# A chunked delta-rule recurrence moved to 64x64 array tiles and interleaved across sequence tiles

## The chip, the cores and the metric

One Trainium2 chip, one of its cores. The metric is the device time of one execution of the whole program in microseconds (us), the median of the runs. All arithmetic of the part that changes is fp32.

## What is computed

The program is a forward pass over 512 tokens of width 1024: a block with an RWKV-7 time mixing beside a differential attention, a cross attention, and further mixers and MLPs. The change touches only the recurrence of RWKV-7, for 8 heads of 64 dimensions:

```
def step(state, inp):
    r_t, w_t, k_t, v_t, kk_t, a_t = inp
    sa = jnp.einsum("bhvk,bhk->bhv", state, -kk_t)
    state = (state * w_t[:, :, None, :]
             + sa[..., None] * (kk_t * a_t)[:, :, None, :]
             + v_t[..., None] * k_t[:, :, None, :])
    y = jnp.einsum("bhvk,bhk->bhv", state, r_t)
    return state, y
```

Both kernels compute it in chunks of 64 tokens. Within a chunk the 64 steps are one linear system per head, a unit triangular 64x64 matrix whose inverse is built by doubling: from blocks of 1 to blocks of 2, 4, 8, 16, 32, 64. The first doubling is a mask; the other five are the "levels" `l = 0..4`, with matrix products. The state passes from chunk to chunk in order.

## The kernel before

Five engines run hand-written streams that wait for each other by counting semaphores. TensorE (the profile's PE) multiplies into eight PSUM banks PB0 to PB7, VectorE (DVE) and ScalarE (ACT) carry results from PSUM to the planes of one large buffer AR, GpSimd (POOL) splits streamed weights for the large projections. A 128 x 512 plane of AR holds, for a tile of 128 tokens, four pairs of heads; `t` is one of the four tiles and has the chunks `c = 2t, 2t+1`; `q` is a head's half of the pair. The helpers `mm` (line 1451) and `tr` (1454) issue one matmul and one transpose; all DVE operations of the stage come from `tt` (line 847), all of ACT's from `f` (line 404), so the trace shows them under lines 1452, 1455, 847 and 404. Each fp32 `mm` is two pairs of records, a weight load and a matmul; I call such a pair a pass. A transpose is one pass.

The recurrence stands between the differential attention and a group norm, with nothing else beside it: a loop over the four tiles, in PE's stream, in DVE's (under `for t in range(TT)`, after three memsets of the state) and in ACT's, each ending in `end_stage()`, where the three engines drain and wait for each other.

Within a tile PE issues: 16 transposes (alpha, v, the decayed beta and k) into PB4 to PB7, which ACT evicts as `TOKA, TOKV, TOKB, TOKK`; 40 products over 64 rows (`head_products` and those for the transposed matrix), which DVE masks into `AQ, BQ, TI, UI`; five levels; `P1`, `TA` and `W1`; the two state steps; and the output `y`, which ACT copies to `HN`. The inverse is kept twice, as `TI` and transposed as `UI`. Both chunks of a head lie as two 64x64 blocks on the diagonal of a 128x128 matrix whose other blocks are zero, so each level multiplies 128x128 matrices, one per head:

```
last = mm(bank4(q, e), AQ[:, h, 0:P], TI[:, h, :])
last = mm(bank4(2 + q, e), UI[:, h, :], XI[:, h, :])
last = mm(bank4(4 + q, e), XI[:, h, :], UI[:, h, :])
```

For half q = 0 and then q = 1, DVE masks the first product to `XI`, and subtracts the other two from `TI` and `UI`. A state step is, for chunk c: read the state `GS[c % 3]` by `TA` (`sa_mm`), form the innovation `SA` on DVE (`sa_ev`), add `TOKK x TOKV` and `TOKB x SA` in PB1 (`gu_mm`), and add the faded state `TG` on DVE (`g_ev`).

Of the kernel before, what the change touches and what calls it, by code (L numbers as in the profile page):

```python
# [20 lines left out]
ACT = mybir.ActivationFunctionType  # L21
# [26 lines left out]
for _name, _n in STREAM:  # L48
# [8 lines left out]
          ("bd_strict", 128), ("bd_incl", 128), ("low_mask", 6 * 128), ("gla_mask", 8 * 128),  # L57
# [32 lines left out]
def constants():  # L90
# [13 lines left out]
    def rope(name, head, width):  # L104
# [5 lines left out]
        for base in range(0, P, width):  # L110
# [13 lines left out]
    same = row // 64 == col // 64  # L124
    put("bd_strict", (same & (row < col)) * 1.0)
    put("bd_incl", (same & (row <= col)) * 1.0)

    low = [((row // (2 * s) == col // (2 * s)) & (row % (2 * s) >= s) & (col % (2 * s) < s)) * 1.0
           for s in (1, 2, 4, 8, 16, 32)]
    put("low_mask", np.concatenate(low, 1))  # L130
# [29 lines left out]
def build(nc, x_d, mem_d, w_d, c_d, v_d, out_d):  # L160
    ctx = ExitStack()
    with ctx:
# [5 lines left out]
        def sb_both(name, shape):  # L168
# [23 lines left out]
                 "ch_trev", "ch_aq", "ch_aqev", "ch_t0ev", "lv_x", "lv_xev", "lv_y", "lv_yev", "w1_mm", "w1_ev", "g_ev", "sa_mm",  # L192
# [74 lines left out]
        AQ, BQ = pk(41, 4, 256), pk(45, 4, 256)  # L267
        TI, UI, XI = pk(49, 2, 128), pk(51, 2, 128), pk(53, 2, 128)
        TOKA, TOKB, TOKK, TOKV = (pk(a, 1, 128) for a in (55, 56, 57, 58))
        BP, KP = pk(59, 1, 128), pk(60, 1, 128)  # L270
        TA, W1, SA, P1 = pk(39, 1, 128), pk(40, 1, 128), pk(18, 1, 128), pk(14 + 7, 1, 128)
        GS = [pk(a, 1, 128) for a in (15, 16, 17)]
        TG = pk(19, 1, 128)

# [118 lines left out]
        def _(act):  # L393
# [140 lines left out]

            for t in range(TT):
                for n, dst in enumerate((TOKA, TOKV, TOKB, TOKK)):
                    act.wait_ge(sems["ch_tr"], 4 * t + n + 1)
                    f(dst, PB[4 + n][:, :].rearrange("p (a n) -> p a n", n=P), ACT.Copy).then_inc(*A.inc("ch_trev"))
                act.wait_ge(sems["w1_mm"], 3 * t + 1)
                f(P1, PB[7][:, :].rearrange("p (a n) -> p a n", n=P), ACT.Copy).then_inc(*A.inc("w1_ev"))  # L540
                act.wait_ge(sems["w1_mm"], 3 * t + 2)
                f(TA, PB[5][:, :].rearrange("p (a n) -> p a n", n=P), ACT.Copy).then_inc(*A.inc("w1_ev"))
                act.wait_ge(sems["w1_mm"], 3 * t + 3)
# [293 lines left out]
        def _(dve):  # L837
# [202 lines left out]

            def two(bank):
                return PB[bank][:, :].rearrange("p (a n) -> p a n", n=256)

            def four(bank):
                return PB[bank][:, :].rearrange("p (a n) -> p a n", n=P)

# [1128 lines left out]
```

## Time and profile before

| what | value |
|---|---|
| median of 3 runs | 2532.34 us (2530.25 to 2533.34) |
| the profiled execution: its time / its span | 2532.6 us / 2530.8 us |
| PE busy | 2306.1 us, 91% of the span |
| DVE, ACT, POOL busy | 1131.1, 583.6, 1192.1 us (45%, 23%, 47%) |
| DMA | 182.52 MB, mean 72 GB/s |

The span goes from the first instruction to the last; the execution's own time is 1.8 us longer. Busy times are of one profiled execution. In a row of the trace, `128*64 128x128` behind a PE operation is the stationary operand (rows*columns) and the moving one (partitions x columns); PEld is the weight load, which has its own column of busy time. The time of a merged row of matmuls ends with the last result, so it is longer than the passes' issue.

### The profile page before, as it was taken

How to read it: one execution, taken by the hardware profiler on the slowest of the kernel's cores; microseconds unless marked ns; L12 is line 12 of the kernel's file. 1: busy time of each engine (PE TensorE's matmuls, PEld its weight loads, DVE VectorE, ACT ScalarE, POOL GpSimd, SP SyncE). 2: the span in 40 equal slices, each digit the busy share in tenths (PEclk: the TensorE clock that was granted, in tenths of full speed). 3: DMA queues.
4: the chain of work that ended last, by engine and by line, in shares of the span. 5: the costliest groups of instructions: out<-in, count | busy, mean ns of one | idle time of the engine just before them, and what ended most of it. 6: DMA issues, size and time to landing. Idle time of an engine off the chain costs nothing.

```text
span 2530.8 us, 28962 instructions
## 1 busy us (share of the span) xinstructions
PE 2306.1 (91%) x11270; PEld 1878.9 (74%) x11270; DVE 1131.1 (45%) x1566; ACT 583.6 (23%) x1161; POOL 1192.1 (47%) x660
## 2 busy tenths in 40 slices
PE   7996788859799999999788779999999998999999
PEld 5763688848678888887466658888887776888887
DVE  6775555552335311336588855311333555530220
ACT  3234200031232200211222152200213554210110
POOL 4550000026625766765223316666665433666665
PEclk9997799989999999999889899999999999999999
DMA  4220000012212232232111102232232121222222
GB/s 185 84 75 17 1 1 1 1 44 99 92 50 79 97 100 93 98 100 84 50 42 42 50 17 82 93 100 95 96 100 84 59 67 36 98 95 96 100 92 90
DMA packets 49641, 182.52 MB, mean 72 GB/s; under 512 B 5504, under 2 KB 5632, under 8 KB 49280
## 3 DMA queue, kind: packets, MB, share of 16 engines
q1 hardware_dynamic: 49248, 179.30, 21.4%
q8 instruction: 72, 1.18, 0.2%
q10 hardware_dynamic: 288, 1.77, 0.2%
q14 instruction: 33, 0.27, 0.0%
HBM read 178.95 MB, written 2.10 MB: 72 GB/s over the span
## 4 chain that ended last, share of the span: by engine, by line
PE 78%; DVE 14%; ACT 5%; issue 2%; POOL 1%; DMA 0%; ACTq 0%; DVEq 0%; SPq 0%; POOLq 0%
PE PB L1488 20%; PE PB L1489 20%; PE PB L1491 20%; PE PB L1452 14%; DVE AR L847 6%; ACT AR L404 4%; PE PB L1455 1%; PE PB L1470 1%; DVE AR L850 1%; PE PB L1545 1%; DVE HN L850 1%; DVE AR L1263 1%; DVE SM L1260 1%; DVE AR L854 1%; DVE SM L890 1%
## 5 line engine op out<-in xcount | busy, mean ns | idle before, releaser
L386 POOL TENSOR_SCALAR WH<-W 128x1024 fp32r<-128x1024 f32 x328 | 354.3, 1080 | 1300.8 <-PE PB L1491 817.9
L1489 PE MATMUL PB<-AR_r,WL 128*128 128x512 f32 (+1 forms) x2496 | 965.8, 388 | 0.0
L388 POOL TENSOR_TENSOR WL<-W,WH 128x1024 fp32r<-128x1024 f32 x328 | 838.0, 2555 | 27.4
L1491 PE MATMUL PB<-AR_r,WH 128*128 128x512 f32 (+1 forms) x2496 | 606.6, 385 | 0.0
L1489 PEld LDWEIGHTS PB<-AR_r,WL 128*128 128x128 f32 x2496 | 476.4, 191 | 100.3 <-issue 7.3
L1491 PEld LDWEIGHTS PB<-AR_r,WH 128*128 128x128 f32 x2496 | 464.1, 189 | 93.0
L1488 PE MATMUL PB<-HN_r,WH 128*128 128x512 f32 x1256 | 511.4, 407 | 0.6 <-POOL WL L388 0.6
L1488 PE MATMUL PB<-AR_r,WH 128*128 128x512 f32 (+1 forms) x1240 | 471.6, 383 | 12.7 <-ACT AR L404 8.1
L1452 PE MATMUL PB<-AR 128*128 128x128 f32 (+6 forms) x2848 | 398.6, 316 | 69.2 <-ACT AR L404 39.9
L1452 PEld LDWEIGHTS PB<-AR 128*128 128x128 f32 (+2 forms) x2848 | 335.6, 201 | 109.4 <-issue 35.8
L404 ACT ACTIVATE AR<-AR 128x512 f32<-128x512 f32 (+4 forms) x278 | 161.0, 616 | 830.3 <-DVE AR L850 729.5
L847 DVE TENSOR_TENSOR H<-H,PB 128x512 f32<-128x512 f32 x80 | 55.0, 687 | 522.3 <-PE PB L1491 485.6
L1488 PEld LDWEIGHTS PB<-HN_r,WH 128*128 128x128 f32 x1256 | 241.0, 192 | 60.8 <-issue 10.5
L850 DVE SCALAR_TENSOR_TENSOR AR<-PB,AR 128x512 f32<-128x512 f32 (+3 forms) x145 | 93.5, 645 | 427.9 <-PE PB L1491 383.1
L1488 PEld LDWEIGHTS PB<-AR_r,WH 128*128 128x128 f32 x1240 | 236.1, 190 | 58.8 <-ACT AR L404 10.1
L847 DVE TENSOR_TENSOR AR<-AR 128x512 f32<-128x512 f32 (+2 forms) x160 | 228.1, 1444 | 45.3 <-ACT AR L404 42.1
L404 ACT ACTIVATE AR<-PB 128x256 f32<-128x256 f32 (+3 forms) x293 | 131.8, 483 | 430.1 <-PE PB L1452 204.2
L847 DVE TENSOR_TENSOR AR_r<-AR,AR_r 128x512 fp32r<-128x512 f32 (+1 forms) x120 | 138.7, 1163 | 12.6 <-ACT AR_r L404 12.6
L1455 PE MATMUL PB<-C,AR 128*128 128x128 f32 x364 | 67.9, 305 | 73.8 <-ACT AR L404 49.1
L1455 PEld LDWEIGHTS PB<-C,AR 128*128 128x128 f32 x364 | 45.6, 153 | 111.1 <-issue 30.6
L1452 PE MATMUL PB<-AR,C 128*128 128x512 f32 x132 | 72.9, 652 | 49.3 <-DVE AR L847 36.9
L404 ACT ACTIVATE AR<-PB,SM 128x128 f32<-128x128 f32 (+3 forms) x128 | 51.0, 447 | 164.6 <-DVE SM L890 87.1
(100 smaller groups left out, 1144.0 us busy)
## 6 DMA issues: line engine op xcount, KB each, us to landing
W<-weights_in SPq DMA_DIRECT2D x328, 512.0 KB, 3.4
C<-constants_in SPq DMA_DIRECT2D x1, 2976.0 KB, 17.1
H<-x_in SPq DMA_DIRECT2D x4, 512.0 KB, 6.8
h_out<-H SPq DMA_DIRECT2D x8, 256.0 KB, 4.4
AR<-mem_in ACTq DMA_DIRECT2D x1, 1024.0 KB, 4.8
V<-vectors_in ACTq DMA_DIRECT2D x1, 703.0 KB, 4.5
C<-constants_in SPq DMA_DIRECT2D x1, 68.0 KB, 3.9
```

Source lines behind the costliest of these rows:

```text
L386: pool.tensor_scalar(WH[:, u % 2, :], w, 1.0, 1.0, ALU.mult, ALU.mult).then_inc(sems["w_round"], 1)
L388: pool.tensor_tensor(WL[:, u % 2, :], w, WH[:, u % 2, :].bitcast(F32), ALU.subtract)\
L404: return act.activation(out, in_, func, **k)
L847: return dve.tensor_tensor(out, a, b, op)
L850: return dve.scalar_tensor_tensor(out, a, scalar, b, op0, op1)
L854: return dve.tensor_scalar(out, a, s1, None, op0)
L890: return dve.tensor_reduce(out, in_, AX.X, op, negate=negate)
L1452: return pe.matmul(out, lhsT, rhs, start=start, stop=stop, **k)
L1455: return pe.transpose(out, in_, cst("ident"))
L1488: pe.matmul(out, lh, rl, start=start and k == 0, stop=False)
L1489: pe.matmul(out, ll, rh, start=False, stop=False)
L1491: ins = pe.matmul(out, lhs(k)[0], rhs(k)[0], start=False, stop=stop and k == KT - 1)
```

## The change

Everything stays fp32 and the stage stays where it is; the other stages are untouched, except that the constants have other masks (5568 columns in the second transfer in place of 5952).

- The two chunks no longer share a 128x128 matrix. Every matmul of the tile's products, the levels, `P1`, `TA`, `W1` and the inner part of `y` is a 64x64 stationary block against 64 moving columns. The inverse `T` of a chunk lies in the partition half opposite to its transpose `U`, so that `corner` (the first product of a level) reads half 1-c and writes half c, and `widen` (the other two) uses all four quadrants of the array. Planes `TU_[t % 2]` and the next hold T and U, `X_` holds 1 - X, `L_` the masked corners.
- `correction` forms 1 - X on DVE from PSUM, and `widen` multiplies T and U by it, so that its results are the new T and U whole; ACT copies them (`level_ev`), T first. `lower` (DVE) masks the level's corner of the matrix in SBUF, ahead of time.
- Operands are doubled by tile parity. The next tile's products (`first_products`, `a_products`, `b_products`) and transposes (`tokens`), and the last tile's state steps (`state_read`, `state_add`) and output (`y_chunk`, `y_state`) stand between the levels. The `end_stage` barriers within the stage are gone, with semaphores in their place.

The diff, cut:

```diff
+        def sub(plane, half, n):
+            return AR[64 * half:64 * half + 64, plane, 64 * n:64 * n + 64]
...
+            def level_ev(t, l):
+                act.wait_ge(sems["lv_tu"], 5 * t + l + 1)
+                if l < 4:
+                    f(AR[:, TU_[t % 2], :], PB[1][:, :], ACT.Copy).then_inc(*A.inc("lv_tev"))
+                f(AR[:, TU_[t % 2] + 1, :], PB[2][:, :], ACT.Copy).then_inc(*A.inc("lv_uev"))
...
+                level_ev(t, 0)
+                level_ev(t, 1)
+                if t < 3:
+                    tokens_ev(t + 1, 0, 7)
+                level_ev(t, 2)
+                if t:
+                    y_evict(t - 1)
+                level_ev(t, 3)
+                if t < 3:
+                    for n in range(1, 4):
+                        tokens_ev(t + 1, n, (7, 3, 7, 5)[n])
+                act.wait_ge(sems["p1_mm"], t + 1)
+                f(P1, PB[6][:, :].rearrange("p (a n) -> p a n", n=P), ACT.Copy).then_inc(*A.inc("p1_ev"))
+                level_ev(t, 4)
+                act.wait_ge(sems["ta_mm"], t + 1)
+                for c in range(2):
+                    f(TA[:, 4 * c:4 * c + 4, :], PB[4 + c][:, 0:256].rearrange("p (a n) -> p a n", n=64), ACT.Copy)\
+                        .then_inc(*A.inc("ta_ev"))
+                act.wait_ge(sems["w1_mm"], t + 1)
+                f(W1, PB[2][:, :].rearrange("p (a n) -> p a n", n=P), ACT.Copy, scale=-1.0).then_inc(*A.inc("w1_ev"))
+            y_evict(TT - 1)
...
+            def first_inverse(t):
+                dve.wait_ge(sems["tu_mm"], t + 1)
+                dst = [AR[:, TU_[t % 2]:TU_[t % 2] + 2, 256 * q:256 * q + 256].rearrange("p k (e n) -> p k e n", n=64) for q in range(2)]
+                for q in range(2):
+                    tt(dst[q], quads(PB[5 + q][:, :], 2), pair_mask("m_low0"), ALU.mult).then_inc(*D.inc())
                 dve.wait_ge(*D.latest)
                 for q in range(2):
-                    tt(heads4(TI, q), eye, heads4(TI, q), ALU.subtract).then_inc(*D.inc("ch_t0ev"))
-                for q in range(2):
-                    tt(heads4(UI, q), AQ[:, q::2, 0:P], pairt, ALU.mult).then_inc(*D.inc())
+                    tt(dst[q], eye24, dst[q], ALU.subtract).then_inc(*D.inc("tu_in"))
+            def lower(t, l):
+                dve.wait_ge(sems["aq_ev"], 2 * t + 2)
+                m = cst("m_up", 64 * l, 64 * l + 64).unsqueeze(1).unsqueeze(1).to_broadcast([P, 2, 4, 64])
+                tt(quads(AR[:, L_[l % 2], :], 2), AR[:, AQ_[t % 2]:AQ_[t % 2] + 2, 0:256].rearrange("p k (e n) -> p k e n", n=64), m,
+                   ALU.mult).then_inc(*D.inc("l_in"))
+            def correction(t, l):
+                dve.wait_ge(sems["lv_x"], 5 * t + l + 1)
+                tt(AR[:, X_, :].rearrange("p (a n) -> p a n", n=64), eye8, PB[0][:, :].rearrange("p (a n) -> p a n", n=64), ALU.subtract)\
+                    .then_inc(*D.inc("lv_xev"))
...
+                fade(c + 1)
+                dve.wait_ge(*D.latest)
+            fade(0)
+            decays(0)
+            first_inverse(0)
+            masked(0, "aq", AQ_[0], (3, 7), "m_strict")
+            lower(0, 0)
+            masked(0, "bq", BQ_[0], (1, 6), "m_strict")
+            for t in range(TT):
+                correction(t, 0)
+                if t:
+                    innovation(2 * t - 2)
+                lower(t, 1)
+                if t < 3:
+                    first_inverse(t + 1)
+                correction(t, 1)
+                if t:
+                    next_state(2 * t - 2)
+                lower(t, 2)
+                if t:
+                    innovation(2 * t - 1)
+                correction(t, 2)
+                lower(t, 3)
+                if t < 3:
+                    decays(t + 1)
+                if t:
+                    next_state(2 * t - 1)
+                correction(t, 3)
+                lower(t, 4)
+                correction(t, 4)
+                if t < 3:
+                    masked(t + 1, "aq", AQ_[(t + 1) % 2], (3, 7), "m_strict")
+                    lower(t + 1, 0)
+                    masked(t + 1, "bq", BQ_[(t + 1) % 2], (1, 6), "m_strict")
+            innovation(6)
+            next_state(6)
+            innovation(7)
...
+            def chunk_products(t, name, banks, ev, *kinds):
+                take(banks[0])
+                take(banks[1])
+                for e in range(4):
+                    for k, (lhs, rhs, swap) in enumerate(kinds):
+                        for c in range(2):
+                            half = 1 - c if swap else c
+                            for q in range(2):
+                                r, o = slice(64 * q, 64 * q + 64), 256 * k + 64 * e
+                                last = mm(PB[banks[q]][64 * half:64 * half + 64, o:o + 64], lhs(e, t)[r, 64 * c:64 * c + 64],
+                                          rhs(e, t)[r, 64 * c:64 * c + 64])
+                last.then_inc(*T.inc(name))
+                free[banks[0]], free[banks[1]] = ev
+            key, query = (lambda p, t: px(K0 + p, t)), (lambda p, t: px(R0 + p, t))
+            def first_products(t):
+                chunk_products(t, "tu_mm", (5, 6), [("tu_in", 2 * t + 2)] * 2, (alpha, beta, True), (beta, alpha, False))
+            def a_products(t):
+                chunk_products(t, "aq_mm", (3, 7), [("aq_ev", 2 * t + 1), ("aq_ev", 2 * t + 2)], (beta, alpha, True), (beta, query, False))
+            def b_products(t):
+                chunk_products(t, "bq_mm", (1, 6), [("bq_ev", 2 * t + 1), ("bq_ev", 2 * t + 2)], (key, alpha, False), (key, query, False))
+            def corner(t, l):
+                pe.wait_ge(sems["l_in"], 5 * t + l + 1)
+                pe.wait_ge(*((sems["tu_in"], 2 * t + 2) if l == 0 else (sems["lv_tev"], 4 * t + l)))
+                take(0)
+                for n in range(8):
+                    for c in range(2):
+                        last = mm(PB[0][64 * c:64 * c + 64, 64 * n:64 * n + 64], sub(L_[l % 2], 1 - c, n), sub(TU_[t % 2], 1 - c, n))
+                last.then_inc(*T.inc("lv_x"))
+                free[0] = ("lv_xev", 5 * t + l + 1)
+            def widen(t, l):
+                pe.wait_ge(sems["lv_xev"], 5 * t + l + 1)
+                if l:
+                    pe.wait_ge(sems["lv_uev"], 5 * t + l)
+                take(1)
+                take(2)
+                u = TU_[t % 2] + 1
+                for n in range(8):
+                    if l < 4:
+                        for c in range(2):
+                            mm(PB[1][64 - 64 * c:128 - 64 * c, 64 * n:64 * n + 64], sub(u, c, n), sub(X_, c, n))
+                    for c in range(2):
+                        last = mm(PB[2][64 * c:64 * c + 64, 64 * n:64 * n + 64], sub(X_, c, n), sub(u, c, n))
+                last.then_inc(*T.inc("lv_tu"))
+                if l < 4:
+                    free[1] = ("lv_tev", 4 * t + l + 1)
+                free[2] = ("lv_uev", 5 * t + l + 1)
...
+            first_products(0)
+            for n in range(4):
+                tokens(0, n, (7, 3, 7, 5)[n])
+            a_products(0)
+            b_products(0)
             for t in range(TT):
...
-                end_stage()
+                corner(t, 0)
+                if t:
+                    state_read(2 * t - 2)
+                widen(t, 0)
+                if t < 3:
+                    first_products(t + 1)
+                corner(t, 1)
+                if t:
+                    state_add(2 * t - 2)
+                widen(t, 1)
+                if t:
+                    state_read(2 * t - 1)
+                corner(t, 2)
+                if t < 3:
+                    tokens(t + 1, 0, 7)
+                widen(t, 2)
+                if t:
+                    state_add(2 * t - 1)
+                    y_chunk(t - 1)
+                corner(t, 3)
+                if t:
+                    y_state(t - 1)
+                widen(t, 3)
+                if t < 3:
+                    tokens(t + 1, 1, 3)
+                    tokens(t + 1, 2, 7)
+                corner(t, 4)
+                if t < 3:
+                    tokens(t + 1, 3, 5)
+                value_terms(t)
+                widen(t, 4)
+                if t < 3:
+                    a_products(t + 1)
+                solved_alpha(t)
+                if t < 3:
+                    b_products(t + 1)
+                solved_values(t)
+            state_read(6)
+            state_add(6)
+            state_read(7)
+            y_chunk(3)
+            y_state(3)
+            pe.wait_ge(sems["y_ev"], 8)
+            for b in range(4):
+                take(b)
             for p in range(4):
```

Where the instructions went. First PE, in the levels of a middle tile, one row per run of equal matmuls (`64x64` is the output, partitions x columns; lv_x and the like are the semaphores waited for). Before, one level:

```order
L1452 MATMUL PB0<-AR 128x128 [waits lv_yev]
L1452 MATMUL PB0<-AR 128x128 x3
L1452 MATMUL PB1<-AR 128x128 [waits lv_yev]
L1452 MATMUL PB1<-AR 128x128 x3
L1452 MATMUL PB2<-AR 128x128 [waits lv_xev]
L1452 MATMUL PB2<-AR 128x128 x3
```

In the change, level 0 of a tile after the first and the first product of level 1:

```order
L1525 MATMUL PB<-AR 64x64 [waits lv_xev,tu_in,l_in]
L1525 MATMUL PB<-AR 64x64 x15
L1525 MATMUL PB<-AR 64x128 [waits aq_ev,ta_ev]
L1525 MATMUL PB<-AR 64x128 x3
L1525 MATMUL PB<-AR 128x128 [waits ch_trev,ta_ev]
L1525 MATMUL PB<-AR 128x128 x3
L1525 MATMUL PB<-AR 64x64 [waits w1_ev,bq_ev,lv_xev]
L1525 MATMUL PB<-AR 64x64 x31
L1525 MATMUL PB<-AR 64x64 [waits bq_ev,ta_ev]
L1525 MATMUL PB<-AR 64x64 x31
L1525 MATMUL PB<-AR 64x64 [waits lv_xev,lv_tev,l_in]
L1525 MATMUL PB<-AR 64x64 x15
```

The state read of the last tile (`64x128`, `128x128`) now lies between a level's first product and its other two, and the next tile's first products behind them.

DVE in the same place. Before, one level:

```order
L847 TENSOR_TENSOR AR<-PB0,C 128x4x128 [waits lv_x]
L847 TENSOR_TENSOR AR<-PB1,C 128x4x128 [waits lv_x]
L847 TENSOR_TENSOR AR<-AR,PB2 128x4x128 [waits lv_y]
L847 TENSOR_TENSOR AR<-AR,PB4 128x4x128 [waits lv_y]
L847 TENSOR_TENSOR AR<-AR,PB3 128x4x128 [waits lv_y]
L847 TENSOR_TENSOR AR<-AR,PB5 128x4x128 [waits lv_y]
```

In the change, the third tile, levels 0 and 1 and what stands between:

```order
L883 TENSOR_TENSOR AR<-C,PB0 128x512 [waits lv_x]
L883 TENSOR_TENSOR AR<-AR,PB3 64x512 [waits sa_mm,w1_ev]
L883 TENSOR_TENSOR AR<-AR,C 128x512 [waits aq_ev]
L883 TENSOR_TENSOR AR<-PB5,C 128x2x256 [waits tu_mm]
L883 TENSOR_TENSOR AR<-PB6,C 128x2x256
L883 TENSOR_TENSOR AR<-C,AR 128x2x256 [waits dve_step]
L883 TENSOR_TENSOR AR<-C,AR 128x2x256
L883 TENSOR_TENSOR AR<-C,PB0 128x512 [waits lv_x]
L883 TENSOR_TENSOR AR<-AR,PB4 64x4x64 [waits gu_mm]
L883 TENSOR_TENSOR AR<-AR,PB4 64x4x64
L883 TENSOR_TENSOR AR<-AR,SM 128x512 [waits g_ev]
L883 TENSOR_TENSOR AR<-AR,C 128x512 [waits aq_ev,dve_step]
```

A level now has one DVE operation that waits for PE and one that does not, and the innovation, the next tile's first inverse and the state's update stand between them.

## Rows read from the trace of the kernel before

**Rows 1.** Busy time by stretch: the four tiles.

```profile
core 0: us, PE busy (x) PEld busy (x) DVE busy (x) ACT busy (x) POOL busy (x), PEclk, DMA share, GB/s
278.20:343.30 65.10, 57.21 (x464) 53.49 (x464) 36.70 (x57) 4.75 (x8) 0.00 (x0) 0.87 0.00 1
343.30:402.40 59.10, 52.16 (x465) 48.95 (x465) 34.59 (x55) 4.45 (x8) 0.00 (x0) 0.97 0.00 1
402.40:461.40 59.00, 52.83 (x463) 49.77 (x463) 34.70 (x54) 3.86 (x7) 0.00 (x0) 0.94 0.01 1
461.40:521.50 60.10, 52.51 (x468) 49.17 (x467) 34.60 (x54) 5.05 (x9) 0.00 (x0) 0.97 0.00 1
```

**Rows 2.** The chain of waits from 285 to 345 us, first tile (start, us, what).

```profile
by line: PE PB L1452 84.7%; DVE AR L847 10.1%; PE PB L1455 2.8%; ACT AR L404 1.0%; ACT HN L404 1.0%; issue 0.7%; ACTq L400 0.1%
...
294.17 32.16 PE PB L1452 x256
```

**Rows 3.** Timeline of PE, second tile (start, us from there, what, xcount, idle before).

```profile
345.26 5.04 PE L1452 MATMUL PB<-AR 64*128 64x128 f32 x64
354.04 31.27 PE L1452 MATMUL PB<-AR 128*128 128x128 f32 x256 [3.75 <-DVE AR L847]
```

**Rows 4.** Timeline from 326.3 to 331.9 us: TA, W1, state read.

```profile
327.09 0.85 PEld L1452 LDWEIGHTS PB<-AR 128*64 128x64 f32 x16 [0.97 <-DVE AR L847]
...
328.11 1.86 PEld L1452 LDWEIGHTS PB<-AR 128*128 128x128 f32 x16 [0.17 <-issue]
...
330.15 0.60 ACT L404 ACTIVATE AR<-PB 128x512 f32<-128x512 f32 x1 [1.32 <-PE PB L1452]
330.80 0.85 PEld L1452 LDWEIGHTS PB<-AR 128*64 128x64 f32 x8 [0.82 <-ACT AR L404]
```

**Rows 5.** Timeline of PE in the differential attention, 214.7 to 217 us.

```profile
214.78 1.12 PE L1452 MATMUL PB<-AR,C 128*128 128x512 f32 x2 [2.29 <-ACT AR L404]
215.84 1.13 PE L1452 MATMUL PB<-AR 64*128 64x512 f32 x4
```

**Rows 6.** Timeline from 327.05 to 327.105 us: the first passes of TA.

```profile
327.09 0.14 PEld L1452 LDWEIGHTS PB<-AR 128*64 128x64 f32 x2 [0.97 <-DVE AR L847]
327.09 0.33 PE L1452 MATMUL PB<-AR 128*64 128x128 f32 x2 [0.78 <-DVE AR L847]
```

**Rows 7.** Groups by line and form, 278.2 to 521.5 us (busy, mean ns | idle before).

```profile
L847 DVE TENSOR_TENSOR AR<-PB,C 128x512 f32<-128x512 f32 x80 | 52.8, 687 | 33.3 <-PE PB L1452 33.2
...
L1452 PE MATMUL PB<-AR 128*64 128x128 f32 x256 | 23.7, 282 | 9.7 <-DVE AR L847 7.0 <-ACT AR L404 2.7
...
L404 ACT ACTIVATE AR<-PB 128x512 f32<-128x512 f32 x28 | 15.7, 600 | 178.4 <-PE PB L1452 172.2 <-PE PB L1455 6.2
...
L847 DVE TENSOR_TENSOR AR<-AR,PB 64x256 f32<-64x256 f32 x16 | 6.7, 419 | 10.6 <-PE PB L1452 10.3
...
L1038 DVE MEMSET AR<- 128x512 f32 x3 | 1.5, 485 | 0.4 <-DVEq L843 0.3
```

**Rows 8.** Groups by line and form of ACT, 530 to 600 us.

```profile
L404 ACT ACTIVATE AR<-PB 128x256 f32<-128x256 f32 x8 | 2.7, 378 | 14.0 <-PE PB L1491 14.0
```

**Rows 9.** Busy time and granted clock by stretch, columns as in rows 1.

```profile
176.50:278.20 101.70, 61.12 (x257) 41.24 (x257) 48.16 (x143) 46.47 (x110) 7.96 (x5) 0.73 0.05 16
1217.60:1500.90 283.30, 227.61 (x1036) 171.38 (x1037) 207.42 (x347) 78.78 (x159) 76.22 (x43) 0.86 0.13 41
1262.00:1272.70 10.70, 10.70 (x38) 7.21 (x36) 6.41 (x11) 5.32 (x8) 0.00 (x0) 0.50 0.10 39
...
350.60:354.00 3.40, 0.00 (x0) 0.00 (x0) 3.35 (x6) 0.00 (x0) 0.00 (x0) 1.00 0.00 0
354.00:357.40 3.40, 3.36 (x15) 3.36 (x16) 0.69 (x1) 0.00 (x0) 0.00 (x0) 0.50 0.00 0
```

**Rows 10.** Timeline of PE, 1262 to 1276 us.

```profile
1266.34 6.51 PE L1452 MATMUL PB<-AR 64*128 64x128 f32 x32
```

More of the change, by code:

```diff
@@ L532, in _, with tokens_ev @@
             end_stage()
[L535 to L547 removed]
+            def tokens_ev(t, n, bank):
+                act.wait_ge(sems["ch_tr"], 4 * t + n + 1)
+                f((TOKA, TOKV, TOKB, TOKK)[n][t % 2], PB[bank][:, :].rearrange("p (a n) -> p a n", n=P), ACT.Copy)\
+                    .then_inc(*A.inc("ch_trev"))
@@ new lines, in tokens @@
+            def tokens(t, n, bank):
+                if n >= 2:
+                    pe.wait_ge(sems["ch_in"], 2 * t + n - 1)
+                take(bank)
+                for p in range(4):
+                    src = (alpha(p, t), px(V0 + p, t), BP[:, p, :], KP[:, p, :])[n]
+                    last = tr(PB[bank][:, tile(p)], src)
+                last.then_inc(*T.inc("ch_tr"))
+                free[bank] = ("ch_trev", 4 * t + n + 1)
+            def chunk_products(t, name, banks, ev, *kinds):
[11 more added lines that the diff above has]
+                free[banks[0]], free[banks[1]] = ev
@@ new lines, in state_read @@
+            def state_read(c):
+                t, r = c // 2, slice(64 * (c % 2), 64 * (c % 2) + 64)
+                pe.wait_ge(sems["ta_ev"], 2 * t + 2)
+                if c:
+                    pe.wait_ge(sems["g_ev"], c)
+                take(3)
+                for p in range(4):
+                    last = mm(PB[3][r, tile(p)], TA[:, 4 * (c % 2) + p, :], GS[c % 3][:, p, :])
+                last.then_inc(*T.inc("sa_mm"))
+                free[3] = ("sa_ev", c + 1)
+                if c < 7:
+                    take(4)
+                    pe.wait_ge(sems["ch_trev"], 4 * t + 4)
+                    for p in range(4):
+                        mm(PB[4][:, tile(p)], TOKK[t % 2][r, p, :], TOKV[t % 2][r, p, :], start=p == 0, stop=False, skip_group_check=True)
@@ new lines, in y_state @@
+            def y_state(t):
+                for p in range(4):
+                    for c in range(2):
+                        last = mm(PB[5 + c][:, 64 * p:64 * p + 64], GS[(2 * t + c) % 3][:, p, :], px(R0 + p, t, 64 * c, 64),
+                                  start=False, stop=True, skip_group_check=True)
+                last.then_inc(*T.inc("y_mm"))
+                free[5], free[6] = ("y_ev", 2 * t + 1), ("y_ev", 2 * t + 2)
+            first_products(0)
+            for n in range(4):
+                tokens(0, n, (7, 3, 7, 5)[n])
```

268 lines of the change are left out of this document (102 added, 166 removed).

## The prediction

> **What bounds the kernel now.** I read the busy times of the page first, then the recurrence alone, since the diff touches nothing else: busy time by stretch, the chain of waits, the timeline. The four tiles take 65.1 + 59.1 + 59.0 + 60.1 = 243.3 us [rows 1], 9.6% of the span, with GpSimd idle throughout and no transfer of weight, so nothing outside can bind. The first tile is longer since it begins at half clock. In all four PE is busy for 52 to 57 us, DVE for 35 to 37, ACT for 4 to 5. The chain that ended last there is 84.7% TensorE and 10.1% VectorE [rows 2]: two halves of four heads alternate, so that PE works on one while DVE carries the other. 256 passes take 31.3 us in the levels [rows 3]. The stage is bound by passes, and a change gains if it makes them cheaper without a longer chain of waits.
>
> **What a pass costs.** 16 passes with 128 loaded columns and 64 moving have loads that take 1.86 us from first to last; without the last one's tail that is 0.112 us each. Eight passes 128*64 with 128 moving columns occupy 0.85 us when all go to one column half: 0.106 each. Sixteen that alternate between the column halves occupy the same 0.85 us [rows 4]. So column halves run at the same time. So do row halves: four passes 64*128 with 512 moving columns take 1.13 us, as long as two passes of full height (1.12) [rows 5]; and 64 passes of 64 rows take 5.0 us, 0.079 each [rows 3]. No row shows a 64x64 block with 64 moving columns, nor four quadrants together. A block of half the size in both directions I take at half of 0.112 and 2 ns: 0.058 us in its quadrant, hence 0.029 with two quadrants, 0.0145 with four. The other bound is the rate at which passes are issued. The steady rate shown is one pass per 0.053 us [rows 4], where the array was the limit, so the issue limit is anywhere below it; two loads and two matmuls begin within 0.015 us at a start [rows 6]. Bounds: 0.0145 and 0.053. I take 0.020, nearest to the start of [rows 6].
>
> **The sum, a middle tile, at full clock and 0.0145.** Passes over four quadrants: next tile's products 192, widen of levels 0 to 3 256, TA 32, y_chunk 64: 544 x 0.0145 = 7.9 us. Over two: corners 160, last widen 32, value terms 32, solved values 32: 256 x 0.029 = 7.4. Unchanged in form: two state reads 16 x 0.109 (0.106 and the gap) = 1.7, the state's updates 32 x 0.112 = 3.6, y_state 16 x 0.112 = 1.8, transposes 16 x 0.109 = 1.7, together 8.8. Before it was 464 passes. New: 18 changes of form of the array; between forms the load waits 0.17 us [rows 4], of which the trace shows a gap and I count 0.15: 2.7. PE has 26.8 us of work, where it had 52.
>
> DVE: 24 operations of 512 columns x 0.687 and four of 0.42 [rows 7] are 18.2 us, where it had 35. ACT: 15 copies x 0.60 [rows 7] and four x 0.38 [rows 8] are 10.5 us, where it had 4.5. Neither binds. But each level is now one chain: corner, the last matmul's own tail 0.17 (its record is 0.28 us, [rows 7], where one starts every 0.109), 0.05 to DVE, correction 0.69, 0.05 to PE, load: 0.95 us; widen, the same way to ACT's copy of T 0.60: 0.90 us. (A hop is 0.04 to 0.05: ACT's copy ends at 330.75 and PE's load starts at 330.80 [rows 4].) Between them lies other work: in level 0 the state read and update term (0.87 + 0.89), then the next products (0.93); in level 1 the update (0.89), but DVE has the next tile's first inverse, four operations or 2.75 us, ahead of that correction: PE waits 1.8; in level 2 transposes (0.44): 0.4 is left; in levels 3 and 4 y_state, transposes and value terms cover it. With 0.2 in small waits: 26.8 + 2.4 = 29.2 us.
>
> The others: lead-in 9.0 (DVE: memsets 1.5 [rows 7], ten operations 6.9, hops 0.6). First tile, without a last tile's work to fill with: five chains of 0.93 + 0.95 + 0.93 + 0.90 = 18.6, products 2.8, value terms, TA and W1 2.3, first inverse 1.8, what of the transposes is not in a wait 0.3: 25.8. Last tile, with no next: 21.6 + 3.8 of waits = 25.4. Tail (two state steps, y, all in series): 10.4. Sum 9.0 + 25.8 + 29.2 + 29.2 + 25.4 + 10.4 = **129 us**; with 0.020 a pass the four-quadrant groups grow by 3.0 us a tile, 11 in all: **140**.
>
> [...]
>
> **The clock.** [...] In the stage now the mean granted clock is 0.87 to 0.97 [rows 1]; it falls after PE has stood still: 350.6 to 354.0 at 1.00 with PE busy 0.00 us, the next 3.4 us at 0.50 [rows 9]. The new stage has no such standstill, but its matmuls are small, and it begins at half. Nearest rows: 0.73 where PE is busy for 60%, 0.86 where for 80% [rows 9]; and from 1262 to 1272.7 PE was busy without a pause, much of it 64-row passes [rows 10], and stayed at 0.50 [rows 9]. PE's calculated busy share is 107 of 140 us, 76%. I take 0.82, between the two, which is 36% of the time at half. If w is the share of the work at half, 224w = 0.36 x (140 + 84w), w = 0.26, and the stage takes 140 + 84 x 0.26 = **162 us**. The time is 2532.6 - 243.3 + 162 = **2451 us**, against the profiled execution's own time; the median of the runs shown is 0.3 below that, which I ignore.
>
> Costed at nothing: the barriers between tiles (0.1 us each); the smaller constants (earlier stages of both kernels wait for them); the weights after the stage, whose ring is full in both kernels; the group norm, whose waits for banks end with y's copies.
>
> **Rivals.**
> - Full clock throughout and the array as the only limit: 129 + 5 for the start at half = 134, **2423**. For: no standstill of PE. Against: [rows 9, 10].
> - Half clock throughout: 224, **2513**. For: quarter-size matmuls, and the 10.7 us of [rows 9]. Against: in the state steps, with 64-row passes, it stayed up (0.97 for the tile, [rows 1]).
> - The issue is the limit, 0.040 to 0.053 a pass: the sum at full clock gives 191 to 231, with the start at half 196 to 236: **2485 to 2525**. For: nothing shown is faster than 0.053. Against: [rows 6].
> - Partial overlap: corner, value terms and solved values write one bank from both row halves, and widen two banks. If row halves exclude each other in a bank, these run at 0.058 and widen at 0.029: 170 at full clock, about 190 with the forecast's clock, **2479**. [...]
> - **Slower than before:** no two 64x64 quadrants overlap. 800 passes x 0.058 = 46.6 us a middle tile, 246 in all, and 6 for the start: 252, **2541**. It decides from about 0.055 us a pass upwards. Against it: both halves overlap singly [rows 4, 5].
>
> **How the numbers follow.** Forecast 0.50 (its own range 2430 to 2475), full clock 0.08, half clock 0.15, issue 0.12, partial overlap 0.10, no overlap 0.05. Range: from 2420, which takes in the full-clock case, to 2514, which takes in half clock; above it lie no overlap (0.05), the upper part of issue (0.04) and some of half clock. Faster by over 0.2% (5 us, about what a measurement of this kernel can tell from no change) needs a stage under 238 us: all but no overlap and the end of issue: 0.94; same 0.01; slower 0.05.
>
> **What would show it.** The timeline of a widen: 64 passes in 0.9 to 1.3 us at full clock (3.7 if nothing overlaps, over 2.6 if issue binds, 1.9 with partial overlap). A corner: 32 passes in 0.93 (1.86 with partial overlap). Stretches by tile: 30 to 40 us each, DVE busy 18, ACT 10.5. The largest wait of PE is for DVE in level 1. The granted clock of the stage 0.75 to 0.9. I am wrong if PE's clock is at 0.5 or 1.0 for nearly all of it, if a pass costs over 0.04, or if anything after the stage moves by more than 2 us.

## Result and profile after

The changed kernel takes 2425.9 us (median of 4 runs, 2424.1 to 2427.1) where the kernel before takes 2532.8 (2530.3 to 2533.5): a ratio of 0.9579, 95% interval 0.9567 to 0.959. The profiled execution has a span of 2424.4 us. The forecast was 2451 with a range from 2420 to 2514, so the time lies inside, near its lower end: 107 us were gained where 82 were forecast.

Busy time by stretch of the changed kernel. The stretches are the lead-in, the four tiles and the tail. The cuts lie where PE begins the first corner of a tile; only the first, at 287.40, lies at the end of the lead-in's passes, 0.76 us before the first corner (288.16). The columns are those of [rows 1].

```profile
277.80:287.40 9.60, 7.59 (x207) 6.63 (x204) 7.13 (x12) 2.39 (x4) 0.00 (x0) 0.71 0.01 2
287.40:314.80 27.40, 21.48 (x771) 19.70 (x767) 13.68 (x22) 8.37 (x16) 0.00 (x0) 0.85 0.02 4
314.80:345.10 30.30, 27.53 (x880) 25.26 (x876) 16.93 (x29) 9.62 (x19) 0.00 (x0) 1.00 0.02 4
345.10:374.90 29.80, 27.72 (x883) 25.37 (x880) 17.03 (x29) 9.62 (x19) 0.00 (x0) 1.00 0.02 4
374.90:401.40 26.50, 23.11 (x685) 21.09 (x680) 11.62 (x20) 7.45 (x15) 0.00 (x0) 1.00 0.02 4
401.40:411.20 9.80, 7.21 (x114) 6.42 (x112) 2.90 (x5) 1.25 (x3) 0.00 (x0) 1.00 0.01 2
sum 133.40, PE 114.64 PEld 104.48 DVE 69.29 ACT 38.71 POOL 0.00; mean PE 19.11 PEld 17.41 DVE 11.55 ACT 6.45 POOL 0.00
```

The stage is 133.4 us long where it was 243.3 [rows 1], 109.9 less. A middle tile takes 30 us in place of 59. From the third row on the granted clock is 1.00 to the end of the stage.

The chain of waits through the two middle tiles (314.8 to 374.9 us), by line, which answers to [rows 2]:

```profile
by line: PE PB L1525 78.2%; DVE AR L883 13.0%; PE PB L1528 5.4%; issue 3.5%
```

It is still TensorE's chain, with VectorE at 13%. The groups of one middle tile (345.1 to 374.9), which answer to [rows 7]; columns as there:

```profile
L1525 PE MATMUL PB<-AR 64*64 64x64 f32 x803 | 18.0, 221 | 2.1 <-DVE AR L883 1.5 <-issue 0.6
L412 ACT ACTIVATE AR<-PB 128x512 f32<-128x512 f32 x15 | 8.3, 598 | 15.5 <-PE PB L1525 12.3 <-PE PB L1528 3.2
L1525 PE MATMUL PB<-AR 64*128 64x128 f32 x32 | 4.6, 285 | 0.0
...
L883 DVE TENSOR_TENSOR AR<-C,PB 128x512 f32<-128x512 f32 x5 | 3.4, 686 | 6.4 <-PE PB L1525 6.4
...
L1528 PE MATMUL PB<-C,AR 128*128 128x128 f32 x16 | 2.4, 283 | 0.0
```

About 800 passes of 64x64 occupy 18.0 us of PE. The timeline of PE shows what one costs. The first row is a corner (32 passes, two quadrants), the second a widen (64 passes, four quadrants):

```profile
338.28 1.15 PE L1525 MATMUL PB<-AR 64*64 64x64 f32 x32
...
354.82 1.16 PE L1525 MATMUL PB<-AR 64*64 64x64 f32 x64 [1.32 <-DVE AR L883]
```

The last pass's own record is 0.22 us of each row. From the first start to the last it is 0.93 us for 31 steps and 0.94 for 63: 0.030 and 0.015 a pass. In the steady part of the trace four passes, one in each quadrant, start every 0.0583 us, 0.0146 each. The row also shows the largest wait of the middle tiles, for DVE in level 1.

Behind the stage something is given back. Counting the matmuls with 512 columns from the program's start, the gain is 109.9 us at the 3000th and 106.35 from the 3300th on. The first row is the stretch of 150 such matmuls from the 3000th on in the kernel before, the second the same work after:

```profile
1198.20:1274.70 76.50, 63.15 (x228) 42.21 (x227) 44.02 (x53) 19.25 (x35) 21.55 (x12) 0.83 0.14 46
```
```profile
1088.30:1166.30 78.00, 64.64 (x227) 43.04 (x226) 43.93 (x52) 19.23 (x35) 21.55 (x12) 0.80 0.15 45
```

Same work on DVE, ACT and GpSimd, 1.5 us longer, with a lower granted clock: 31.2 us at half clock where it was 26.4. The next 150 lose another 2.0, with 9.8 us at half clock for 7.7 (0.92 after, 0.93 before); that can account for 1.0 of them at most, so the rest has no explanation here. Of 109.9 gained, 106.4 are left.

### The profile page after: what moved, and what is told of

Read it like the earlier page. It is cut to its first block, busy times and chain, and to the rows that moved or that the text cites. A ratio compares the mean times of both kernels' runs of the same rounds, so it can differ in the third digit from the quotient of the medians.

```text
span 2424.4 us, 32302 instructions
## 1 busy us (share of the span) xinstructions
PE 2207.1 (91%) x12918; PEld 1782.8 (74%) x12918; DVE 1060.8 (44%) x1460; ACT 603.8 (25%) x1205; POOL 1193.7 (49%) x660
## 4 chain that ended last, share of the span: by engine, by line
PE 78%; DVE 14%; ACT 5%; issue 2%; POOL 1%; DMA 0%; ACTq 0%; DVEq 0%; SPq 0%; POOLq 0%
PE PB L1561 21%; PE PB L1562 21%; PE PB L1564 21%; PE PB L1525 11%; DVE AR L883 5%; ACT AR L412 4%; PE PB L1528 1%; DVE AR L886 1%; PE PB L1543 1%; PE PB L1618 1%; DVE HN L886 1%; DVE AR L1336 1%; DVE SM L1333 1%; DVE AR L890 1%; DVE SM L926 1%
## 5 line engine op out<-in xcount | busy, mean ns | idle before, releaser
L1525 PE MATMUL PB<-AR 64*64 64x64 f32 (+4 forms) x4496 | 297.9, 261 | 64.4 <-ACT AR L412 37.9
L1525 PEld LDWEIGHTS PB<-AR 64*64 64x64 f32 (+3 forms) x4496 | 238.8, 160 | 101.3 <-issue 39.9
L412 ACT ACTIVATE AR<-PB 128x512 f32<-128x512 f32 (+3 forms) x333 | 151.9, 491 | 328.9 <-PE PB L1564 175.5
```

What stands on the lines that cost most here:

```text
L412: return act.activation(out, in_, func, **k)
L1525: return pe.matmul(out, lhsT, rhs, start=start, stop=stop, **k)
```

## Experiments

Stage times below run from DVE's first memset of the stage to the first matmul of the group norm, as the 133.4 us of the changed kernel. Each kernel in the first three experiments differs from the changed one by the edit shown alone.

**1. The order alone.** The interleaving is undone.

```diff
-corner(t, 0); state_read(2t-2); widen(t, 0); first_products(t+1); corner(t, 1); ...
+for l in range(5):
+    corner(t, l)
+    if l == 4: value_terms(t)
+    widen(t, l)
+solved_alpha(t); solved_values(t)
+state_read(2t); state_add(2t); state_read(2t+1); state_add(2t+1); y_chunk(t); y_state(t)
+first_products(t+1); tokens(t+1, 0..3); a_products(t+1); b_products(t+1)
```

> The interleaving alone is undone: quadrant passes and double buffers stay as in the changed kernel, but all state steps, y and the next tile's products of a tile come behind its levels, one after the other. Theory (each level is a chain of two hops to DVE and ACT, about 1.6 us in which PE has nothing of its own, and the interleaved work fills that): the stage grows from 133 us by about 32 us at full clock (5 x 4.4 us of levels, 10.2 of state, 7.7 of products a tile, in place of 29.9), so 165 us and 2458 us of time; if PE's standstills also bring the clock down, more, up to 2490. Rival (the gain is nearly all cheaper passes, the interleaving hides what was cheap): stage 133 to 140 us, 2426 to 2433.

```profile
278.30:438.40 160.10, 114.73 (x3504) 102.74 (x3498) 69.73 (x113) 39.02 (x76) 0.00 (x0) 0.98 0.01 3
```

The stage takes 160.1 us and the kernel 2447.2. PE's work is the same (114.7 us busy), and between corner and widen it now waits 1.0 us from start to start each way. So the interleaving is worth 27 us of the 110, the theory's mechanism with 5 us less than its size. The other 83 (243.3 to 160.1) belong to the rest of the change: the smaller passes, with about half of DVE's work and without the barriers. This experiment doesn't split them. The clock did not fall for these waits. The time is 11 us below the forecast, since the stage is 5 us shorter than forecast and nothing was given back behind it: that part is 2.3 us shorter than in the kernel before, where it is 3.9 longer in the changed kernel.

**2. Overlap of quadrants, and the clock.** The passes are the same, in another order inside each group: one quadrant after the other, and, in a second kernel, the two column halves of one row half alternating. The widen, in the first:

```diff
-for n in range(8):
-    for c in range(2): mm(PB[1]..., sub(u, c, n), sub(X_, c, n))
-    for c in range(2): mm(PB[2]..., sub(X_, c, n), sub(u, c, n))
+for c in range(2):
+    for n in range(8): mm(PB[1]..., sub(u, c, n), sub(X_, c, n))
+    for n in range(8): mm(PB[2]..., sub(X_, c, n), sub(u, c, n))
```

and in the second:

```diff
-for n in range(8):
-    for c in range(2): mm(PB[1]..., sub(u, c, n), sub(X_, c, n))
-    for c in range(2): mm(PB[2]..., sub(X_, c, n), sub(u, c, n))
+for c in range(2):
+    for n in range(8):
+        mm(PB[1]..., sub(u, c, n), sub(X_, c, n))
+        mm(PB[2]..., sub(X_, c, n), sub(u, c, n))
```

> The same 64x64 passes in another order: in each group all passes of one quadrant stand in a row, then those of the next. Theory (the cheapness is overlap of quadrants whose passes stand next to each other in PE's queue; alone a quadrant takes 0.058 us a pass): a widen of 64 passes takes 3.7 us where it takes 0.94, a corner 1.86 where it takes 0.93, the stage about 250 us, the time 2543 us. Rival 1 (the engine deals passes to quadrants from further down its queue, or 0.0146 is an issue rate that has nothing to do with quadrants): widen stays at 0.94, time 2426. On the clock: if it follows how much of the array works, it falls to 0.50 for most of the stage and a widen takes 7.5 us (over 2700 us); if it follows PE's standstills, it stays at 1.00, since PE is busy without a pause.

> The changed kernel with its four-quadrant groups issued by row halves: first all passes of one row half, alternating between its two column halves, then the other. Theory (overlap of neighbours in the queue, two quadrants at a time): a widen takes 1.9 us where it takes 0.94, the stage at full clock 158 us and 4 for its start, 162, the time 2455. On the clock, which fell to 0.50 with one quadrant at a time although PE was never idle and stayed at 1.00 with four: if half of the array is enough it stays at 1.00 and these numbers hold; if not, the stage is 190 to 250 us, 2485 or more.

The stage of the kernel with one quadrant at a time, then of the one with two:

```profile
279.10:586.40 307.30, 295.23 (x3504) 281.70 (x3500) 69.73 (x113) 39.22 (x76) 0.00 (x0) 0.58 0.01 2
```
```profile
279.70:451.20 171.50, 157.77 (x3505) 146.80 (x3503) 69.66 (x113) 38.93 (x77) 0.00 (x0) 0.84 0.01 3
```

The times are 2600.6 and 2462.6 us. Rival 1 falls: only the order in the queue differs, and with one quadrant at a time the kernel is 67 us slower than before the change. Most of what the stage grew by is the clock, though. It was at half for 256 of the 307 us; if all of that was time of PE, and took 1.78 times as long as at full clock, as the widen below, an estimated 195 us of stage would be left at full clock, about 60 more than the changed kernel needs. A widen with one quadrant at a time, in a stretch at half clock, reads

```profile
330.32 5.99 PE L1525 MATMUL PB<-AR 64*64 64x64 f32 x64 [0.78 <-DVE AR L883]
```

where 0.94 us from first start to last was 5.68 here. Another widen of the same run stands at full clock, from its first start to its last (columns as in [rows 1]):

```profile
502.99:506.18 3.19, 3.19 (x65) 3.19 (x64) 0.37 (x1) 0.00 (x0) 0.00 (x0) 1.00 0.00 0
```

3.19 us: 0.051 a pass, not 0.058. Within a run its passes start 0.058 to 0.059 us apart, as the theory had it, but around a change of quadrant 0.004 to 0.055: the end of one run and the start of the next overlap, which the theory had left out.

With two quadrants a widen at full clock takes 1.91 us, as forecast:

```profile
312.31 1.91 PE L1525 MATMUL PB<-AR 64*64 64x64 f32 x64 [0.78 <-DVE AR L883]
```

The clock is a surprise. With one quadrant at a time it was at half for most of the stage, as one of the two cases on record had it, but with two it went neither way that I had written. PE was busy for 96% of the stage with one quadrant at a time, 92% with two and 86% with four, and the mean granted clock was 0.58, 0.84 and 0.95. So the kernel with the busiest PE had the lowest clock. What brings it down isn't shown. It isn't the number of quadrants alone: in their reordered groups both kernels work in one row half of the array at a time, and in experiment 6 a run over two quadrants in different row halves held full clock for 30.5 us. Nor are waits excluded. With one quadrant at a time the clock fell at 368.4, 440.0 and 508.3 us, each time within 1.2 us behind a wait of PE (0.55, 0.55 and 0.73 us idle); but the waits of 1.32 us in the changed kernel brought no fall. In the serial order of experiment 1, with four quadrants and PE waiting between groups, the mean was 0.98.

**3. DVE's order in level 1.** The first inverse of the next tile moves behind the corrections.

```diff
 lower(t, 1)
-first_inverse(t + 1)
 correction(t, 1)
 next_state(2 * t - 2)
 lower(t, 2)
+inverse_mask(t + 1)
 innovation(2 * t - 1)
 correction(t, 2)
+first_inverse(t + 1, mask=False)
```

> The first inverse of the next tile on DVE moves from before the correction of level 1 to after it: its two masks behind the mask of level 2, its two subtractions behind the correction of level 2. Theory (PE's wait of 1.3 to 1.6 us per tile in level 1 is DVE's order alone): this wait goes in three tiles, a new one of 0.3 to 0.5 us comes before the widen of level 2, and the stage is 3.5 to 5 us shorter: 128 to 130 us, the time 2421 to 2423. Rival (DVE's work is only moved, and PE waits for it as long in level 2, at the correction or at the innovation that stands behind the masks): stage within 1 us of 133, time 2425 to 2427.

The stage takes 129.0 us, 4.4 less, and the time is 2420.1. PE's waits for DVE in the stage, in the changed kernel and here:

```profile
PE PB L1525 <- DVE AR L883: 9.1, 10, 2.4
```
```profile
PE PB L1534 <- DVE AR L883: 6.6, 10, 1.2
```

The longest wait halves. In level 1 of the third tile the step from the state's update to the widen is now 0.20 us, a change of form and no more, where it was 1.60. The theory holds, and the stage has its size. But the middle tiles gained only 1.0 and 0.9 us each. 2.5 of the 4.4 lie in the first tile, which also had 3.4 us at half clock where the changed kernel has 7.3, so not all of it is the wait.

**4. State products as blocks.** The state is block-diagonal, but its outer products are computed as 64x128 passes of which half is unused.

```diff
-mm(PB[4][:, tile(p)], TOKK[r, p, :], TOKV[r, p, :], ...)
+for v in (slice(0, 64), slice(64, 128)):
+    o = p * P + v.start
+    mm(PB[4][v, o:o + 64], TOKK[r, p, v], TOKV[r, p, v], ...)
```

> The outer products of the state (keys by values, and the update by the innovation) are computed as their two used 64x64 diagonal blocks, in the two column halves of one row half, instead of as 64x128 passes of which half is unused: 16 passes of 0.029 us in place of 8 of 0.126, and one change of form less. Theory (PE is the path in the middle tiles): about 1.4 us less of PE a chunk, of which the model keeps 6.7 us over the stage: 126 us, the time 2419. Rival (levels are bound by their hops to DVE and ACT by now, so that PE waits where it worked): under 2 us, stage 131 to 133, time 2424 to 2426.

The stage takes 130.0 us: half of the expected 7. The time, 2418.8, is as forecast, but by luck, since the part behind the stage came out 5.3 us shorter than in the changed kernel. Two things are large enough to have taken the rest in the stage. In level 1 of the third tile PE had less of its own beside the wait of experiment 3, and the clock fell behind it:

```profile
351.20:354.60 3.40, 1.67 (x74) 1.31 (x71) 3.30 (x7) 0.00 (x0) 0.00 (x0) 1.00 0.02 5
354.60:358.00 3.40, 3.40 (x41) 3.07 (x43) 1.66 (x3) 1.09 (x2) 0.00 (x0) 0.51 0.00 0
```

The other is experiment 6. Computing y's state part in blocks as well was not tried.

**5. Both edits together, and more.** The first kernel joins experiments 3 and 4. The second adds the state reads as blocks, each row half with a bank of its own. The third is the first with useless passes in PE's waits of the first tile.

```diff
 # second: state_read, then innovation
-last = mm(PB[3][r, tile(p)], TA[:, 4 * (c % 2) + p, :], GS[c % 3][:, p, :])
+for b, v in ((3, slice(0, 64)), (7, slice(64, 128))):
+    o = p * P + v.start
+    last = mm(PB[b][r, o:o + 64], TA[v, 4 * (c % 2) + p, :], GS[c % 3][v, p, v])
-tt(SA[r], W1[r], four(3)[r], ALU.subtract)
+for b, v in ((3, slice(0, 64)), (7, slice(64, 128))):
+    tt(SA[r, :, v], W1[r, :, v], four(b)[r, :, v], ALU.subtract)
 # third: in the first tile, behind corners 0 to 3 and widens 1 and 2 (behind corner 2: range(2))
+for k in range(6):
+    for c in range(2): mm(PB[4][64*c:64*c+64, ...], C[64*c:64*c+64, ...], C[64*c:64*c+64, ...])
```

> Both edits of the runs before together: outer products in 64x64 blocks, the next tile's first inverse behind the corrections of levels 1 and 2. Theory (each alone left a wait that the other takes away, and the half-clock stretch that the block version had in the middle of the second tile came from PE's wait of 1.2 us in level 1): middle tile 26.4 us at full clock, no half clock there, the stage 122 to 124 us where the changed kernel has 133.4, the time 2414 to 2418. Rival (the clock falls because there is less work in PE's time): a half-clock stretch in the middle tiles again, 125 us or more, the time 2418 or more.

> The version before it, and the state reads too as 64x64 blocks, each row half in a bank of its own, with the innovation on DVE in two operations of 256 columns. Theory (PE is still the path): 0.35 us and a change of form less per chunk, 2 us over the stage, 120 to 122 us, the time 2412 to 2416. Rival (from here DVE and the hops set the pace, and the innovation is 0.15 us longer): no shorter than the version before it, within 1 us.

> The version with blocks and the later inverse, and in the first tile passes without use (24 of 64x64 in two quadrants, 0.7 us, into a bank that is not in use) in seven of PE's waits of about 1 us. Theory (the half clock in the first tile follows PE's waits there; the version without them has 7 to 10 us at half in the lead-in and first tile): one half-clock stretch less there, the stage 1 to 2.5 us shorter. Rival (it is inherited from the stage before, or passes of half the array do not count): clock as without them, stage equal or up to 1 us longer.

| kernel | stage, us | time, us | ratio to before (95%) |
|---|---|---|---|
| changed kernel | 133.4 | 2425.9 | 0.9579 (0.9567 to 0.959) |
| both edits | 127.1 | 2418.8 (5 runs) | 0.9542 (0.9525 to 0.9558) |
| and reads as blocks | 125.4 | 2419.4 (5 runs) | 0.9553 (0.9539 to 0.9567) |
| both edits and filler | 126.8 | 2420.2 (one run) | |

Both edits together beat the changed kernel by 6.3 us of stage and 7 us of time. Against the blocks alone (2418.8, one run) the time shows no gain, and it lies just above the forecast 2414 to 2418. The half clock in the third tile (the text on record calls it the second) is gone, as the theory said. But 122 to 124 was expected: the middle tiles take 29.1 and 28.4 us, not 26.4, and half clock came up at the tail instead (the last 10.4 us at 0.66). The reads as blocks save 1.7 us of stage, near the forecast 2, and show no further gain in time. The filler stood in six waits, not in the seven of the text on record, and tells nothing of the clock: with DVE's order mended, nothing was left at half in the first tile behind 288.5 us for it to act on.

**6. PE stands still in the middle of groups.** The chain above has 3.5% of "issue", time in which PE waits for nothing that the profile shows. In the changed kernel it is at such rows, inside the first corner of a tile:

```profile
309.42 5.61 PE L1525 MATMUL PB<-AR 64*64 64x64 f32 x263
316.27 7.31 PE L1525 MATMUL PB<-AR 64*64 64x64 f32 x209 [1.24 <-issue]
```

Four such stops cost it 3.0 us (1.46, 0.58, 0.41 and 0.57 from start to start). In the kernel with both edits seven cost 6.4, and an eighth in the last tile 0.8. From stop to stop lie, in the kernel with both edits, 252, 253, 378 or 505 passes, 2, 3 or 4 times 126, and a pass is two instructions, a matmul and its load. Its instruction queue from 300 to 400 us:

```profile
q8 instruction: 24, 0.39, 1.6%
```

That is 24 packets of 16 KB, 4.2 us apart on average; the closest two of the stage begin 3.4 us apart, at 337.35 and 340.78 us. At 0.0146 a pass 126 passes last 1.84 us. So the suspicion was instruction fetch, a block of 16 KB for about 126 passes and their waits; the 3.6 to 4 us a block in the two texts below was my estimate. The test puts 1024 useless passes in a row behind the changed kernel's last y, over four quadrants and over two:

```diff
 y_state(3)
+for k in range(128):
+    for c in range(2):
+        for q in range(2):
+            mm(PB[1 + c][64*q:64*q+64, ...], C[64*c:64*c+64, ...], C[64*c:64*c+64, ...])
```

> Behind the last y products of the changed kernel stand 1024 more passes of 64x64 over all four quadrants, which nothing uses, in one run and with no wait inside. [...] Theory (instruction fetch: PE eats a block of about 126 passes in 1.84 us at 0.0146 and gets one in 3.6 to 4): the burst goes at 0.0146 for the first one to three blocks, then stops at each block, and takes 22 to 30 us; the time grows by 21 to 29 us. Rival (the stops are something of the recurrence, a bank or a buffer): 1024 x 0.0146 = 15.0 us without a stop, of which 1.0 lies beside the copies of y; the time grows by 14 us.

> The same 1024 passes, but over the two quadrants of the diagonal, 0.029 us a pass. Theory (fetch, a block in 3.6 to 4 us): 126 passes take 3.7 us here, as long as a block needs to come, so the burst takes 30 to 33 us, nearly as long as with four quadrants, with no stop or short ones. Rival (no limit of fetch): 30 us, twice the time of four quadrants.

PE's timeline through the burst over four quadrants, then over two:

```profile
410.08 3.72 PE L1525 MATMUL PB<-C 64*64 64x64 f32 x239
417.09 2.91 PE L1525 MATMUL PB<-C 64*64 64x64 f32 x128 [3.29 <-issue]
420.55 2.50 PE L1525 MATMUL PB<-C 64*64 64x64 f32 x128 [0.54 <-issue]
424.00 2.09 PE L1525 MATMUL PB<-C 64*64 64x64 f32 x128 [0.95 <-issue]
427.73 2.09 PE L1525 MATMUL PB<-C 64*64 64x64 f32 x128 [1.64 <-issue]
431.18 2.09 PE L1525 MATMUL PB<-C 64*64 64x64 f32 x128 [1.36 <-issue]
434.64 2.09 PE L1525 MATMUL PB<-C 64*64 64x64 f32 x128 [1.36 <-issue]
```
```profile
411.11 30.59 PE L1525 MATMUL PB<-C 64*64 64x64 f32 x1024
```

From the second row on PE stops after exactly 128 passes each time, 256 instructions. The last two blocks begin 3.46 us apart, 0.0270 us a pass, where the array takes 0.0146. (The second and third rows are longer because the clock was at half from 418.1 to 421.5 us, behind the stop of 3.3 us: four passes start every 0.107 us there, every 0.058 before and after.) The burst takes 28.3 us over four quadrants and 30.4 over two: nearly no difference. For the run over two, theory and rival both had about 30 us, so it decides nothing about fetch. But it held full clock throughout; columns as in [rows 1]:

```profile
411.11:441.60 30.49, 30.40 (x1025) 30.10 (x1024) 0.00 (x0) 1.94 (x3) 0.00 (x0) 1.00 0.12 38
```

The DMA queues of the first (414 to 438 us) show what comes in meanwhile:

```profile
q8 instruction: 7, 0.11, 2.0%
```

Seven blocks, 0.11 MB, one for each stop. The rival (15.0 us without a stop) is out.

The last run puts half a block of passes into the first tile of the kernel with both edits:

```diff
+filler(5)  # behind corner 0, and behind corner 1; filler(6) behind widen 1; 4 passes each step
```

> The version with blocks and the later inverse, with 64 passes without use in PE's waits of the first tile, half a block of instructions. Theory (PE stops where a block of its instruction stream ends): the stops behind the first tile, which came at passes 964, 1217, 1469, 1847, 2100, 2730 and 3069 of the stage without them, stay on the same raster of about 126 passes (964 + 126k), and so lie at other places of the program, half a block earlier. Rival (they belong to places of the program): they move by 64 with the program, to 1028, 1281, 1533 and so on. The stage takes 125 to 129 us either way.

Counted from the stage's first pass, PE stops in the kernel with both edits at 967, 1220, 1472, 1850, 2103, 2355, 2733 and 3238, and with 64 passes more in the first tile at 968, 1221, 1851, 2104, 2230, 2733 and 2860. Each lies on one raster of 126, not 64 further on. The changed kernel, whose second tile has 32 passes fewer than that with both edits, stops at 967, 1850, 1976 and 2732, on the same raster. (The time with the 64 passes more is 2418.4.) So the stops go by the count of PE's instructions, one packet of 16 KB for each in the burst, and not by a place of the program.

In the kernel before, no wait for issue in the stage is longer than 0.3 us, with 14 such packets in 243.3 us, 17 us apart. At 0.0146 us a pass the stops are there.

## Why the prediction came out as it did

**What a pass costs: right.** The estimate from loads and halves was 0.0145 with four quadrants and 0.029 with two; the traces show 0.0146 and 0.029 to 0.030. The overlap is real and hangs on the order in the queue: the same passes took 0.051 in runs by quadrant (experiment 2).

**The issue term: mis-sized.** The step "I take 0.020, nearest to the start" added 11 us. Neighbouring passes start 0.006 to 0.007 us apart in the steady part, so no steady issue rate binds. There is a limit of supply behind it, 0.027 us a pass over a long run, which shows only as 3.0 us of stops: with the waits and the slower forms between the groups the stage took a block every 4.8 us (28 from 278 to 412 us), the long run one every 3.46.

**The clock term: mis-sized, and the larger error.** The step "I take 0.82, between the two" added 22 us. The mean over the stage was 0.95, outside the 0.75 to 0.9 that I had named, and 1.00 from 302 us on, so that one of my signs of being wrong nearly came true. The two rows that I took it from, 60 and 80% of PE busy, were chosen by busy time; in experiment 2 the kernels with a busier PE had the lower clock. The row that I used against full clock, 10.7 us at half with 64-row passes [rows 9, 10], stayed without an explanation of its own. No run shows the 224 us of the sum, a stage wholly at half clock: the nearest, with one quadrant at a time, was at half for 256 of 307 us, and a widen took 5.68 us there at half and 3.19 at full, 1.78 times as long.

**The sum by tiles: right within 2 us each.** In full clock it gave 9.0 + 25.8 + 29.2 + 29.2 + 25.4 + 10.4 = 129; measured were 9.6, 27.4, 30.3, 29.8, 26.5 and 9.8, 133.4. Of the 4.4 us more, 2.2 lie in the first two stretches, which have 13.7 us at half clock, and 2.8 in the next three, which have the four stops with 3.0; the tail is 0.6 shorter. So it is the rival "full clock throughout", with 134, to which I gave 0.08, that came closest to what happened. The forecast's own range, 2430 to 2475, misses the time; the wide range holds it because its lower end was set for that rival. The two mis-sized terms made the stage 28.6 us too long (162 for 133.4), and the 3.6 us given back behind it hide a part of that.

**The waits: right.** PE waits for DVE in level 1, 1.6 us from start to start where 1.8 was forecast, and moving DVE's first inverse takes it away (experiment 3). DVE was busy 17 us a tile for 18 forecast, ACT 9.6 for 10.5. Going from 64x64 to another form costs 0.15 us from start to start, back to 64x64 0.20.

**The rivals.** "Partial overlap" is out: a corner writes one bank from both row halves, in disjoint partitions, at 0.030 a pass, where it has 0.058. "No overlap" put the kernel at 2541. With one quadrant at a time it took 2600.6: the passes cost less than that rival had them (0.051 for 0.058), but the clock fell, which it hadn't reckoned with.

**"Wrong if anything after the stage moves by more than 2 us": it did,** by 3.6 us between the 3000th and the 3300th matmul and 3.9 in all. That more of the same work ran at half clock is what the rows show; why there, stays open. In the eleven kernels of the experiments the part behind the stage came out between 2.9 us shorter and 3.8 longer than before, so a difference of a few us in the time alone says little about an edit of the stage.

## What to carry over

Count what a pass costs from the array's geometry, and let neighbours in the queue go to different quadrants; the same passes in runs by quadrant lost more than the whole gain (2600.6 us, against 2425.9 and 2532.8 before), the larger part of it by the clock. When passes get four times cheaper, look for the next supply behind them: here PE's instructions, one block of 256 in 3.46 us, so a pass that saves array time by becoming two costs fetch (3.0 us of stops in the changed kernel, 6.4 with both edits). And read "issue" in a chain of waits by counting instructions between the stops.

## What the hardware showed that I had not expected

- In the long run of experiment 6 PE's instructions arrived at one 16 KB block per 3.46 us. A run of 64x64 passes over four quadrants held 0.0146 us a pass for 239 passes and, with its stops, 0.0270 in the blocks after that at full clock.
- The mean granted clock in the same stage, with the same instructions, was 0.58, 0.84 and 0.95 with one, two and four quadrants at a time, while PE's busy share fell from 96 to 86%. The two quadrants lay in one row half; over two in different row halves PE held full clock for 30.5 us. The cause isn't shown.
- Two quadrants of different row halves write one bank in disjoint partitions at 0.030 us a pass (a corner), as two with a bank each (1024 passes in 30.4 us).
- Executions of one kernel can differ by more than one edit is worth: the version with both edits ran from 2410.9 to 2420.0 us. Only one of them is profiled, so the cause isn't shown.
